# Sample rows in the first prompt pass, weights in 1 MB blocks of 512 columns, and one K projection per head pair

## The chip, the cores and the metric

The kernel runs on the 8 cores of one Trainium2 chip. The batch is divided over them: each core has one prompt of 2048 rows and 16 sample sequences of 4 rows, and all weights. The cores don't talk to each other. The metric is the device time of the slowest core in microseconds (us), as the median of the runs shown.

## The reference

A two-layer decoder step with model width D = 2048 and MLP width 8192, run for a prompt group and for a sample group with the same weights.

```python
# layer 0, recurrent
gate, xr = split(rmsnorm(h) @ w_in, 2)              # w_in (2048, 4096)
xr = causal_conv(xr, conv_state, conv_w, conv_b)    # 4 taps
r, i = sigmoid(block_diag(xr, wa) + ba), sigmoid(block_diag(xr, wx) + bx)   # 16 blocks of 128x128
a = exp(-8 * r * softplus(-lam)); u = sqrt(1 - a * a) * (i * xr)
h_t = a_t * h_(t-1) + u_t                           # scan over time
h = h + (gelu(gate) * hs) @ w_out
h = h + square(relu(rmsnorm(h) @ w_up0)) @ w_dn0    # (2048, 8192), (8192, 2048)
k, v = split(rmsnorm(h) @ w_kv, 2)                  # 4 heads of 64 each; w_kv (2048, 512)
# layer 1, attention over the last 128 positions, with a sink logit per head; 32 query heads of 64
q = rmsnorm(h) @ w_q
p = exp(q k^T / 8 - m) / (sum + exp(sink - m))      # 8 query heads share one k, v head
h = h + (p @ v) @ w_o
h = h + square(relu(rmsnorm(h) @ w_up1)) @ w_dn1
y = rmsnorm(h)
```

The prompt begins with zero states. The sample rows take a convolution state, a recurrent state and a K/V cache of 128 rows for each of the sequences. Outputs are y for both groups, the new states, and the new K and V rows.

## The kernel before

Activations are kept transposed in SBUF: features on the 128 partitions in 16 chunks, rows on the free axis. A pass carries T rows through both layers. `run_pass` (line 492) is called five times: passes 0 to 3 take 512 prompt rows each, pass 4 the core's 64 sample rows (`is_s`, T = 64). The residual stream is `hres` in float32, the bf16 input of the matmuls `xn`; everything else of a pass is laid out by hand in one big tile `U` (class `UV`, line 224).

Matmuls have a 128 x 128 block of weights as the stationary operand and T columns of activations as the moving one. `mm_group` (358) issues a whole accumulation: 16 matmuls for an inner dimension of 2048, 64 for the down-projection. A pass has 5376 such matmuls: 512 of w_in, 256 each of w_out, w_q and w_o, and 1024 each of two up- and two down-projections. `gemm_to_h` (432) does w_out and w_o and adds them to `hres`; `mlp` (445) does up and down: after an up matmul VectorE does relu and the norm's factor (455), ScalarE the square (458). `post_chunk` (416) follows each new chunk of `hres` with its square on ScalarE (376) and, two chunks later, a matmul with ones that sums the squares (380).

The weights come in 85 blocks per pass of 2 MB in bf16 (list `blocks`, 290 to 312; a w_dn block is 8192 rows by 128 columns, the others 2048 by 512, w_in as two parts of 256). There are three slots, `wslot`. `w_acquire` (344) is called before a block is used, and issues loads up to two blocks ahead on the Pool queue; a load waits until the matmuls that read its slot are done. The weights in HBM are float32 and the load casts them. A block with number bi divisible by 3 is read so in pass 0 only, the others in passes 0 and 1; on the last such time SP also stores the bf16 block to the scratch tensor `wscr` (354), from which later passes load it without a cast (333). Of the 425 block loads 141 cast and 284 come from `wscr`; 85 blocks are stored.

The recurrent stage (732 to 743) is a software pipeline over 16 chunks: matmuls of chunk i, then on VectorE the scan of chunk i-3 (708) and the convolution of chunk i-1 (666), its gate matmuls (686) and activations (694). The K projection (785 to 800) computes each of 4 heads twice, once for either half of the partitions, with 64-column weight blocks: 128 matmuls. V (801 to 809) has rows as the stationary operand and streams all 512 columns of w_kv, of which the K half is used only for the last block of the prompt. Attention (`attn_unit`, 856) goes over 32 units of two chunks (four heads) and 128 queries: scores for one or two key blocks (872), exp on ScalarE (878), values and sums of the exponentials (900), and on VectorE sum plus sink (912), reciprocal (916) and two multiplies (918). Each unit is finished before the next is issued. The sample pass has its own attention (937 to 1032), one unit for each of 16 sequences.

Each engine executes its instructions in the order of the program. Dependences are tracked by names of tiles in `Prog`, and become semaphore waits.

The softmax here doesn't subtract the row's maximum and nothing guards it: scores larger than these inputs give would overflow.

## Time and profile before

| what | us |
|---|---|
| median of 3 runs | 7713.69 |
| fastest, slowest of them | 7228.85, 7719.43 |
| profiled execution: span of the slowest core (2) | 7383.0 |
| profiled execution: span of the fastest core (5) | 7094.3 |
| TensorE matmul busy, core 2 | 6128.0 |
| VectorE, ScalarE, GpSimd busy, core 2 | 1823.3, 1561.3, 514.3 |

The profile is of one execution, for which no time other than the spans of its cores is shown. A span goes from the first to the last instruction of a core; a time also has what lies around it. Matmuls overlap, so the mean duration of one (some 400 ns) is not its cost in a stream. "Granted clock" is the share of TensorE's full clock that the chip let through.

### The profile page before, as it was taken

What the parts mean: (1) busy time and instruction counts of PE and PEld (TensorE: products, weight loads), DVE (VectorE), ACT (ScalarE), POOL (GpSimd) and SP (SyncE); (2) the same over time, 40 slices, a digit from 0 to 9 for tenths busy, and PEclk for the clock granted to TensorE, in tenths of its full rate; (3) what the DMA queues carried; (4) which work ended last, traced back from release to release, by engine and by line L of the source; (5) the groups of instructions that cost most, each with busy time, mean ns of one, the idle gap of its engine ahead of it and who ended that gap; (6) DMA issues with size and microseconds to landing.
All of it is one profiled execution on the core that took longest, in us unless ns stands there. A gap on an engine that the chain in (4) does not pass through costs nothing.

```text
span 7383.0 us, 82123 instructions; the slowest of 8 cores (7094.3 to 7383.0 us)
## 1 busy us (share of the span) xinstructions
PE 6128.0 (83%) x32728; PEld 2982.2 (40%) x33176; DVE 1823.3 (25%) x3379; ACT 1561.3 (21%) x2520; POOL 514.3 (7%) x608
## 2 busy tenths in 40 slices
PE   6778788786887888897899989979999899973665
PEld 3333343333333344333344444443444444433545
DVE  6210052102611043103620151035110331023121
ACT  6310012101711012101711031026110121015121
POOL 1002100021001100010000000000000000000000
PEclk8887899898999999888999999977888888875666
DMA  9999959999899957996334313333333123335849
GB/s 157 141 144 139 154 93 130 139 158 178 174 196 200 202 151 143 204 190 176 119 150 151 122 69 149 148 114 113 115 126 125 70 80 126 117 139 172 311 140 332
DMA packets 728559, 1118.41 MB, mean 151 GB/s; under 512 B 467188, under 2 KB 676596, under 8 KB 676596
## 3 DMA queue, kind: packets, MB, share of 16 engines
q0 software_dynamic: 691056, 892.38, 58.7%
q1 hardware_dynamic: 37128, 220.76, 9.0%
q8 instruction: 269, 4.41, 0.2%
q14 instruction: 106, 0.87, 0.0%
HBM read 1213.33 MB, written 196.51 MB: 191 GB/s over the span
## 4 chain that ended last, share of the span: by engine, by line
PE 58%; DMA 21%; issue 7%; DVE 7%; ACT 5%; POOL 1%; another core or an unknown queue 0%; DVEq 0%; ACTq 0%; POOLq 0%; SPq 0%
PE psum L364 53%; DMA sb_wslot<-w_up 9%; DMA sb_wslot<-w_dn 6%; DMA sb_wslot<-wscr 4%; DVE sb_U L916 2%; PE psum L793 1%; POOL sb_wslot L111 1%; DMA sb_wslot<-w_in 1%; PE psum L900 1%; DVE sb_xn L547 1%; ACT sb_U L878 1%; DMA wscr<-sb_wslot 1%; ACT L701 1%; PE psum L380 1%; DVE sb_U L402 1%
## 5 line engine op out<-in xcount | busy, mean ns | idle before, releaser
L364 PE MATMUL psum<-sb_xn,sb_wslot 128*128 128x512 bf16 (+1 forms) x13859 | 2793.4, 368 | 395.3 <-DMA sb_wslot<-w_up 205.1
L364 PE MATMUL psum<-sb_U,sb_wslot 128*128 128x512 bf16 (+1 forms) x12589 | 2575.9, 369 | 336.7 <-DMA sb_wslot<-w_dn 158.2
L364 PEld LDWEIGHTS psum<-sb_xn,sb_wslot 128*128 128x128 bf16 x14080 | 1290.2, 107 | 1883.7 <-issue 978.7
L364 PEld LDWEIGHTS psum<-sb_U,sb_wslot 128*128 128x128 bf16 x12800 | 1167.9, 106 | 1716.1 <-issue 967.9
L455 DVE SCALAR_TENSOR_TENSOR sb_relu_t<-psum,sb_rstd 128x512 f32<-128x512 f32 (+1 forms) x640 | 382.7, 598 | 1919.3 <-PE psum L364 1904.0
L458 ACT ACTIVATE sb_U<-sb_relu_t 128x512 bf16<-128x512 f32 (+1 forms) x640 | 355.2, 556 | 1976.9 <-DVE sb_relu_t L455 1966.8
L376 ACT ACTIVATE sb_sqst<-sb_hres 128x512 bf16<-128x512 f32 (+1 forms) x320 | 177.8, 556 | 2621.8 <-DVE sb_hres L465 2199.3
L465 DVE TENSOR_TENSOR sb_hres<-sb_hres,psum 128x512 f32<-128x512 f32 (+1 forms) x160 | 95.2, 595 | 2233.0 <-PE psum L364 2062.3
L101 POOL DMA_DIRECT2D sb_wslot<-wscr x284 | 151.7, 534 | 4209.1 <-PE psum L364 2439.9
L111 POOL DMA_DIRECT2D sb_wslot<-w_dn x212 | 242.7, 1155 | 917.0 <-issue 489.4
L916 DVE RECIPROCAL sb_U<-sb_U 128x256 f32<-128x256 f32 x128 | 224.4, 1753 | 13.5 <-DVE sb_U L912 0.5
L440 DVE TENSOR_TENSOR sb_hres<-sb_hres,psum 128x512 f32<-128x512 f32 (+1 forms) x160 | 95.2, 595 | 454.7 <-PE psum L364 411.7
L408 ACT ACTIVATE sb_xn<-sb_hres,sb_vecs 128x512 bf16<-128x512 f32 (+1 forms) x280 | 173.7, 632 | 127.8 <-PE psum L364 127.8
L878 ACT ACTIVATE sb_U<-psum 128x512 bf16<-128x512 f32 x248 | 136.4, 595 | 227.1 <-PE psum L872 227.0
L900 PE MATMUL psum<-sb_U,sb_Vpad 128*128 128x128 bf16 x992 | 80.1, 226 | 117.4 <-ACT sb_U L878 117.4
L364 PE MATMUL psum<-sb_U,sb_wgate 128*128 128x512 bf16 (+1 forms) x156 | 45.6, 366 | 150.6 <-DVE sb_U L655 88.8
L678 DVE SCALAR_TENSOR_TENSOR sb_U<-sb_U,sb_vecs 128x512 f32<-128x512 f32 (+1 forms) x240 | 157.9, 658 | 26.1 <-DVE sb_U L678 0.9
L380 PE MATMUL psum<-sb_sqst,sb_onesb 128*128 128x512 bf16 (+1 forms) x316 | 110.4, 359 | 23.6 <-ACT sb_sqst L376 23.3
L364 PE MATMUL psum<-sb_wslot,sb_xn 128*4 128x512 bf16 (+1 forms) x504 | 125.1, 415 | 0.9 <-issue 0.7
L111 POOL DMA_DIRECT2D sb_wslot<-w_up x53 | 60.7, 1145 | 891.7 <-PE psum L364 572.0
L900 PEld LDWEIGHTS psum<-sb_U,sb_Vpad 128*128 128x128 bf16 x992 | 60.3, 100 | 137.3 <-issue 137.3
L649 ACT ACT_TABLE_LOAD x75 | 96.2, 1283 | 74.2 <-PE psum L364 72.7
(136 smaller groups left out, 2733.7 us busy)
## 6 DMA issues: line engine op xcount, KB each, us to landing
sb_wslot<-wscr POOLq DMA_DIRECT2D x284, 2048.0 KB, 9.4
wscr<-sb_wslot SPq DMA_DIRECT2D x85, 2048.0 KB, 14.0
sb_wslot<-w_up POOLq DMA_DIRECT2D x53, 2048.0 KB, 36.1
sb_wslot<-w_dn POOLq DMA_DIRECT2D x212, 512.0 KB, 20.8
sb_wslot<-w_in POOLq DMA_DIRECT2D x26, 1024.0 KB, 31.0
sb_U<-xp SPq DMA_DIRECT2D x16, 1024.0 KB, 9.4
yp<-sb_U SPq DMA_DIRECT2D x16, 1024.0 KB, 4.1
sb_wslot<-w_out POOLq DMA_DIRECT2D x7, 2048.0 KB, 24.1
```

What stands on the lines that cost most here:

```text
L101: self.q[eng].append((waits, lambda e: e.dma_start(out=out, in_=in_), sem, 16))
L111: self.q[eng].append((waits if i == 0 else [], (lambda e, out=out, in_=in_: e.dma_start(out=out, in_=in_)), sem, 16))
L364: ins = e.matmul(out_ap, lhsT=l, rhs=r, start=(i == 0), stop=(i == n - 1))
L376: P.op("act", lambda e: e.activation(out=sq_ap, in_=hres[:, c, 0:T], func=AF.Square), reads=[("h", c)], writes=sq_keys)
L380: P.op("pe", lambda e: e.matmul(psum[:, bank, 0:T], lhsT=onesb[:], rhs=sq_ap, start=(c == 0), stop=(c == NCH - 1)), reads=["onesb"] + sq_k ...
L408: P.op("act", lambda e: e.activation(out=xn[:, c, 0:T], in_=hres[:, c, 0:T], func=AF.Copy, scale=vcol(gv, c)), reads=[("h", c)] + CONST_R, ...
L455: P.op("dve", lambda e, r=r, bank=bank: e.scalar_tensor_tensor(out=relu_t[:, r, 0:T], in0=psum[:, bank, 0:T], scalar=0.0, in1=rstd[:, 0:T] ...
L458: P.op("act", lambda e, r=r, m=m: e.activation(out=hid[m].ap, in_=relu_t[:, r, 0:T], func=AF.Square), reads=[("relu", r)], writes=hid[m].keys)
L678: P.op("dve", lambda e, j=j: e.scalar_tensor_tensor(out=tv(xc.ap), in0=sh_(j), scalar=vcol(V_CW0 + j, c), in1=tv(xc.ap), op0=ALU.mult, op1 ...
L878: P.op("act", lambda e, bank=bank, nk=nk, pt=pt: e.activation(out=pt.ap[0:nk, 0:ncol], in_=psum[0:nk, bank, 0:ncol], func=AF.Exp, scale=0. ...
L900: ins = e.matmul(psum[:, bank, off + ci * nq:off + (ci + 1) * nq], lhsT=lhsT, rhs=Pt[s][kb].ap[0:nk, j * nq:(j + 1) * nq], start=first, st ...
L916: P.op("dve", lambda e: e.reciprocal(out=dn.ap[:, 0:wo], in_=dn.ap[:, 0:wo]), reads=dn.keys, writes=dn.keys)
```

## The change

- The fifth pass is gone. Pass 0 carries the 64 sample rows beside its 512 prompt rows (`S = (pi == 0)`), in tiles of their own (`hres_s`, `xn_s`, `Us`). In `mm16`, which replaces `mm_group`, each stationary block is used twice: for 64 sample columns, into a bank that four chunks share, and then for the 512 prompt columns.
- A weight block is 1024 rows by 512 columns, 1 MB in bf16, for w_dn also; 170 blocks a pass. There are four slots of half the size (4 x 8 KB a partition instead of 3 x 16 KB). `w_pair` acquires two blocks and issues the loads of the next two. The down-projection accumulates four output chunks in four banks over four pairs. The rule for the scratch copy (number divisible by 3) is kept.
- K is projected once per pair of heads, with 128-column weight blocks: 32 matmuls instead of 128; VectorE writes each head to both halves. V streams 256 columns, except for the last block of the prompt.
- Attention is split in `attn_scores` and `attn_pv`, and the scores of the next unit are issued before the values of this one. In pass 0 a sample sequence is worked on between units (`smp_a`, `smp_b`, `smp_c`), every second unit one. The new V rows of the samples go through a scratch tensor `vscr`.
- `rec_sample` does the recurrence of the sample rows four chunks at a time, inside the pipeline of pass 0, in memory of `K2T` and `Us`. The start of pass 0 also loads and transposes the sample inputs and states (`load_T`), and the new states are transposed out after w_out.

```diff
-NSLOT = 3
+NSLOT = 4
+NS = 64
...
-        for pi in passes:
-            for cp in range(8):
-                add_block([(w_in[:, cp * 256:(cp + 1) * 256], 0, 256), (w_in[:, D + cp * 256:D + (cp + 1) * 256], 256, 256)], 16, 512)
...
-            for b in range(16):
-                add_block([(w_dn[0][:, b * 128:(b + 1) * 128], 0, 128)], 64, 128)
...
+    def add_k2048(w, col_parts):
+        for kh in range(2):
+            blocks.append([(w[kh * 1024:(kh + 1) * 1024, c0:c0 + n], off, n) for (c0, off, n) in col_parts])
...
+            for b in range(4):
+                for kb in range(8):
+                    blocks.append([(w_dn[layer][kb * 1024:(kb + 1) * 1024, b * 512:(b + 1) * 512], 0, 512)])
...
+        def w_pair():
+            i = wstate["next"]
+            wstate["next"] += 2
+            while wstate["issued"] < min(len(blocks), i + NSLOT):
+                w_issue(wstate["issued"])
+                wstate["issued"] += 1
...
+        def mm16(wv, wk, c0, rhs, rkeys, out_ap, bank, rhs_s=None, out_s=None, bank_s=None, rkeys_s=(), start=True, stop=True,
+                 start_s=True):
+            for kh in range(2):
+                def fn(e, kh=kh):
+                    ins = None
+                    for k in range(kh * 8, kh * 8 + 8):
+                        l = wv(k, c0, 128)
+                        if rhs_s is not None:
+                            e.matmul(out_s, lhsT=l, rhs=rhs_s(k), start=(start_s and k == 0), stop=(stop and k == 15),
+                                     skip_group_check=True)
+                        ins = e.matmul(out_ap, lhsT=l, rhs=rhs(k), start=(start and k == 0), stop=(stop and k == 15),
+                                       skip_group_check=True)
+                    return ins
...
+            for b in range(4):
+                banks = [next_bank(hold=True) for _ in range(4)]
+                bs_ = next_bank(hold=True) if S else None
+                for q in range(4):
+                    wv, wk = w_pair()
+                    for j in range(4):
+                        mm16(wv, wk, j * 128, lambda k, q=q: hid[q * 16 + k].ap, lambda k, q=q: hid[q * 16 + k].keys,
...
+                if S and i < NCH and i % 4 == 3:
+                    rec_sample(i // 4)
...
+            for gp in range(2):
+                bank = next_bank()
+                bs_ = next_bank() if S else None
+                mm16(wv, wk, gp * 128, XN[0], XN[1], psum[:, bank, :], bank, XNS[0] if S else None,
+                     psum[:, bs_, 0:NS] if S else None, bs_, XNS[1])
...
+            for ui, un in enumerate(units):
+                s = attn_scores(*un)
+                if S:
+                    if ui % 2 == 0:
+                        smp_a(ui // 2)
+                    else:
+                        smp_b(ui // 2)
+                if prev is not None:
+                    attn_pv(*prev)
+                prev = (s,) + un
+                if S and ui % 2 == 0 and ui > 0:
+                    smp_c(ui // 2 - 1)
```

## Rows read from the trace of the kernel before

**Rows 1.** Spans and mean granted clock of the cores.

```profile
core 2: 7383.0 us, clock 0.854
...
core 5: 7094.3 us, clock 0.898
```

**Rows 2.** Core 2 by passes: engines' busy us (instructions), granted clock, DMA share, GB/s.

```profile
0.00:1782.00 1782.00, 1399.00 (x6437) 644.31 (x6550) 416.40 (x677) 334.38 (x488) 225.56 (x205) 0.89 1.06 142
1782.00:3432.00 1650.00, 1381.75 (x6580) 646.03 (x6692) 410.08 (x671) 337.68 (x497) 154.78 (x151) 0.91 0.97 186
3432.00:4891.00 1459.00, 1335.62 (x6581) 637.82 (x6693) 410.14 (x672) 337.97 (x498) 45.18 (x85) 0.95 0.35 129
4891.00:6595.00 1704.00, 1585.56 (x6600) 703.39 (x6711) 414.06 (x674) 341.68 (x501) 45.19 (x85) 0.80 0.29 109
6595.00:7383.00 788.00, 426.02 (x6537) 350.69 (x6535) 172.57 (x688) 209.57 (x538) 43.55 (x82) 0.60 0.66 236
```

**Rows 3.** The same columns for core 0, its passes 0 and 3.

```profile
0.00:1781.00 1781.00, 1605.89 (x6551) 696.54 (x6552) 418.45 (x677) 335.65 (x489) 225.65 (x205) 0.79 1.04 142
...
4917.00:6364.00 1447.00, 1327.26 (x6709) 633.49 (x6708) 410.50 (x674) 339.28 (x500) 45.19 (x85) 0.97 0.35 128
```

**Rows 4.** Weight loads as Pool issues them, in order of time (start us, us).

```profile
267.28 1.14 POOL L111 DMA_DIRECT2D sb_wslot<-w_up  x1 [13.32 <-PE psum L380]
...
558.84 4.58 POOL L111 DMA_DIRECT2D sb_wslot<-w_dn  x4 [21.79 <-PE psum L364]
...
865.00 1.15 POOL L111 DMA_DIRECT2D sb_wslot<-w_kv  x1
...
977.45 1.14 POOL L111 DMA_DIRECT2D sb_wslot<-w_q  x1 [18.96 <-PE psum L364]
991.25 1.14 POOL L111 DMA_DIRECT2D sb_wslot<-w_o  x1 [12.66 <-PE psum L364]
...
3661.44 0.53 POOL L101 DMA_DIRECT2D sb_wslot<-wscr  x1 [14.15 <-PE psum L380]
...
3886.77 0.53 POOL L101 DMA_DIRECT2D sb_wslot<-wscr  x1 [13.28 <-PE psum L364]
```

**Rows 5.** DMA issues: count, KB each, median us from issue to landing.

```profile
sb_wslot<-wscr POOLq DMA_DIRECT2D x284, 2048.0 KB, 9.4
...
sb_wslot<-w_up POOLq DMA_DIRECT2D x53, 2048.0 KB, 36.1
...
sb_wslot<-w_q POOLq DMA_DIRECT2D x6, 2048.0 KB, 19.7
```

**Rows 6.** TensorE in order of time in pass 4 (start us, us, count).

```profile
7173.13 0.67 PE L364 MATMUL psum<-sb_U,sb_wslot 128*128 128x64 bf16 x16
...
7173.67 0.69 PE L364 MATMUL psum<-sb_U,sb_wslot 128*128 128x64 bf16 x16
...
7188.26 3.57 PE L364 MATMUL psum<-sb_xn,sb_wslot 128*128 128x64 bf16 x64 [3.30 <-DMA sb_wslot<-wscr]
```

**Rows 7.** Attention of pass 2, 4247 to 4344: groups by line, busy us, mean ns.

```profile
L916 DVE RECIPROCAL sb_U<-sb_U 128x256 f32<-128x256 f32 x32 | 56.1, 1753 | 3.3
...
L900 PE MATMUL psum<-sb_U,sb_Vpad 128*128 128x128 bf16 x256 | 19.8, 221 | 29.8 <-ACT sb_U L878 29.8
...
L918 DVE TENSOR_TENSOR sb_U<-psum,sb_U 128x128 bf16<-128x128 f32 x63 | 15.5, 287 | 3.3
...
L912 DVE TENSOR_TENSOR sb_U<-psum,sb_dvec 128x256 f32<-128x256 f32 x32 | 13.6, 425 | 5.8 <-PE psum L900 5.8
```

**Rows 8.** Sample attention on VectorE, groups of the whole span.

```profile
L1025 DVE RECIPROCAL sb_U<-sb_U 128x64 f32<-128x64 f32 x16 | 8.8, 553 | 1.8 <-DVE sb_U L1021 0.2
...
L1028 DVE TENSOR_TENSOR sb_U<-psum,sb_U 64x64 bf16<-64x64 f32 x32 | 7.1, 222 | 2.2
...
L972 DVE CAST sb_U<-sb_U 128x512 bf16<-128x512 f32 x16 | 6.8, 423 | 0.5
```

**Rows 9.** Recurrent stage of pass 0, columns as in rows 2.

```profile
62.00:242.00 180.00, 131.84 (x552) 56.65 (x563) 117.19 (x209) 123.98 (x143) 14.85 (x13) 0.86 1.03 148
```

More of the change, by code:

```diff
@@ L349, in w_acquire @@
                 wstate["issued"] += 1
-            parts, kc, nct = blocks[i]
-            s = i % NSLOT
-            pord, bi = divmod(i, NBLK)
-            if pord == conv_pass(bi) and pord < len(passes) - 1:
-                P.dma("sp", wscr[bi], wslot[s][:, :], s_ws[s], reads=[("ws", s, j) for j in range(4)], writes=[("wscr", bi)])
-            view = wslot[s][:, 0:kc * nct].rearrange("p (k n) -> p k n", k=kc)
-            return view, [("ws", s, j) for j in range(4)]
-        def mm_group(out_ap, bank, pairs, reads):
-            n = len(pairs)
+            views = []
@@ new lines, in w_pair @@
+            keys = []
+            for ii in (i, i + 1):
+                s = ii % NSLOT
+                pord, bi = divmod(ii, NBLK)
+                if pord == conv_pass(bi) and pord < len(passes) - 1:
+                    P.dma("sp", wscr[bi], wslot[s][:, :], s_ws[s], reads=[("ws", s)], writes=[("wscr", bi)])
+                views.append(wslot[s][:, :].rearrange("p (k n) -> p k n", k=8))
+                keys.append(("ws", s))
+            return (lambda k, c0, n: views[k // 8][:, k % 8, c0:c0 + n]), keys
@@ new lines, in mm16 @@
+        def mm16(wv, wk, c0, rhs, rkeys, out_ap, bank, rhs_s=None, out_s=None, bank_s=None, rkeys_s=(), start=True, stop=True,
[11 more added lines that the diff above has]
+                    return ins
+                rd = [wk[kh]] + [kk for k in range(kh * 8, kh * 8 + 8) for kk in rkeys(k)]
+                wr = [("ps", bank)]
+                if rhs_s is not None:
+                    rd += list(rkeys_s)
+                    wr.append(("ps", bank_s))
+                P.op("pe", fn, reads=rd, writes=wr)
@@ L361, in fn, with post_s @@
+        def post_s(b, xg):
+            P.op("act", lambda e: e.activation(out=sqst_s[:], in_=hres_s[:, 4 * b:4 * b + 4, :].rearrange("p c t -> p (c t)"),
+                                               func=AF.Square), reads=["h_s"], writes=["sqst_s"])
+            if xg is not None:
+                scale_gs(xg, 4 * b, 4)
+            bank = stats["bank_s"]
             def fn(e):
                 ins = None
-                for i, (l, r) in enumerate(pairs):
-                    ins = e.matmul(out_ap, lhsT=l, rhs=r, start=(i == 0), stop=(i == n - 1))
@@ L432, in gemm_to_h, with h_add @@
-        def gemm_to_h(T, rhs_chunk, rhs_keys, post=None):
+                for j in range(4):
+                    ins = e.matmul(psum[:, bank, 0:NS], lhsT=onesb[:], rhs=sqst_s[:, j * NS:(j + 1) * NS],
+                                   start=(b == 0 and j == 0), stop=(b == 3 and j == 3))
+                return ins
+            P.op("pe", fn, reads=["onesb", "sqst_s"], writes=[("ps", bank)])
+        def h_add(m, bank):
+            P.op("dve", lambda e: e.tensor_tensor(out=hres[:, m, :], in0=hres[:, m, :], in1=psum[:, bank, :], op=ALU.add),
+                 reads=[("h", m)], writes=[("ps", bank), ("h", m)])
@@ new lines, in h_add_s, with post_tail @@
+        def h_add_s(b, bank):
+            P.op("dve", lambda e: e.tensor_tensor(out=hres_s[:, 4 * b:4 * b + 4, :].rearrange("p c t -> p (c t)"),
+                                                  in0=hres_s[:, 4 * b:4 * b + 4, :].rearrange("p c t -> p (c t)"),
+                                                  in1=psum[:, bank, 0:256], op=ALU.add),
+                 reads=["h_s"], writes=[("ps", bank), "h_s"])
+        def post_tail(S):
+            for m in range(NCH - DEFER, NCH):
+                stats_mm(m)
+            stats_finish(S)
```

1087 lines of the change are left out of this document (577 added, 510 removed).

## Prediction

> **What bounds the kernel now.** I read the cores first: core 2 spans 7383.0 us at a mean granted clock of 0.854, core 5 only 7094.3 at 0.898 [rows 1]. Then I cut core 2 at the first output issue of each pass, which gives five stretches [rows 2]: 1782, 1650, 1459, 1704 and 788 us. The reader should see two kinds of pass. Passes 2 and 3 are bound by TensorE: in pass 2 it is busy 1336 of 1459 us while the DMA engines are used at 0.35. Passes 0 and 1 do the same matmuls with DMA share 1.06 and 0.97 and take 323 and 191 us longer: there the float32 weights are read and cast. Pass 4 has one eighth of the rows, yet moves all weights again at 236 GB/s and takes 788 us, at a granted clock of 0.60. Pass 3 is longer than pass 2 by its clock alone: 0.80 against 0.97 for core 0 in its pass 3, which took 1447 us [rows 3].
>
> The weight queue shows the same by blocks [rows 4]. In pass 0 the first up-projection issues 16 blocks in 291.6 us (267.28 to 558.84), 18.2 each, and the down-projection 16 in 306.2, 19.1 each. In pass 2 it is 16 in 225.3, or 14.1, which is TensorE's pace (64 matmuls). In pass 0 the query and output projections too go at TensorE's pace, 13.8 us (977.45 to 991.25), since three slots let them run ahead. A block of w_up lands 36.1 us after its issue, with two or three in flight; one of w_q, nearly alone, after 19.7; one from the bf16 copy after 9.4 [rows 5].
>
> **The change, part by part,** against core 2's span of 7383.
>
> Fifth pass. From 6595 only the output of pass 3 remains; 18 us for it is an estimate (four issues and one landing). Removed: 788 - 18 = 770.
>
> Sample columns in pass 0. Each of 5376 large matmuls gets a 64-column one ahead of it with its own weight load. In pass 4 such pairs of load and matmul run from 7173.13 to 7173.67, sixteen of a group and one for the statistics, which is 32 to 33 ns each; after a DMA wait, at the lower clock, 64 take 3.57 us or 55 ns [rows 6]. I take 33 ns, since here a 512-column matmul stands between them. A block costs 14.1 + 64 x 0.033 = 16.2 us. The bounds are nothing (load and matmul in the shadow of the DMA wait) and 5376 x 55 ns = 296 us, if all is exposed.
>
> Slots and blocks. Two pairs replace three blocks, so the load of pair n+1 starts when pair n-1 has been used, and has one pair's matmuls to hide behind. When a load takes longer than that, two loads overlap in flight, and the queue has nothing for the time from a free slot to the first data. Call that 3 us, an estimate from two issues of 1.14 us [rows 4] and their signals. With P the matmuls of a pair and C the transfer (18.2, the pace of w_up), a pair takes (P + 3 + C) / 2 = (16.2 + 3 + 18.2) / 2 = 18.7 us in pass 0. That is +0.5 for each of 32 up blocks, -0.4 for each of 32 down blocks (19.1 before; their rows of 512 bytes become 2 KB, as w_up has), and +4.6 for each of the 13 of w_out, w_kv, w_q and w_o. Sum 16 - 13 + 60 = +63. Pass 1 has 191 / 85 = 2.2 us a block over pass 2, so C about 16.6; (14.1 + 3 + 16.6) / 2 = 16.9, +0.3 for 64 blocks and +2.8 for 13: about +55, of which I take 48, as some of those blocks hide behind attention. In passes 2 and 3 a pair lands in 9.4 us and has 14.1: nothing, and once that cover is gone (a landing above 14) half the excess per pair. The bounds of this step are 0, where 18.2 was only the old queue's pace, and the price in the second rival.
>
> The 512-byte rows of w_dn cost 5% against w_up's (19.1 to 18.2). The Trainium skill ("DMA: Bandwidth & Descriptors", Specifications) asks for at least 512 bytes per transfer for line rate, since below it the engine reads, modifies and writes; the cast rows of w_dn land as 256 bytes. By that rule alone the down stage would gain far more than the 13 us above. The trace agrees in sign only.
>
> K and V. K takes 32 instead of 128 matmuls a pass, at 0.216 us by the pace of the projections (13.8 / 64): 96 x 0.216 = -21. V streams 256 instead of 512 columns: 64 x 0.108 = -7. At clock 0.80 this is -35 in pass 3. The eight VectorE multiplies for K stay and hide behind V's matmuls.
>
> Attention. Scores of the next unit now go ahead of this unit's values, which looks like 29.8 us saved per pass, TensorE's wait for the exponential. But the unit is bound by VectorE: over 32 units its three groups are busy 13.6 + 56.1 + 15.5 = 85.2 us of some 92 [rows 7], and one unit needs 0.42 + 1.75 + 2 x 0.29 = 2.75 us. I take -3 a pass; bounds 0 and 92 - 85 = 7. In pass 0 a sample rides on every second unit and adds VectorE 0.42 + 0.55 + 4 x 0.22 = 1.85 us [rows 8], times 16 samples: +30.
>
> Recurrence of pass 0: between 62 and 242 VectorE is busy 117.19 of 180 us [rows 9]. Four sample groups add some 42 small operations each at 0.2 to 0.3 us (the L1028 kind), 42 us in all. VectorE runs in order, and the prompt chunk queued behind a group waits, with its gate matmuls behind it. Half is hidden by the wait for w_in: +20, bounds 0 and 42.
>
> Start and end of pass 0: twelve groups of transposes with copies and one normalization before the first matmul, +12; new transposes out, +17; both estimates from copies of 0.2 to 0.4 us, bounds 0 and 60. Reads of vscr wait for its write, many units ahead: nothing.
>
> Sums: pass 0 1782 + 63 + 12 + 20 + 30 - 3 - 28 + 17 = 1893; pass 1 1650 + 48 - 31 = 1667; pass 2 1459 - 31 = 1428; pass 3 1704 - 38 = 1666; end 18. Span 6672, 711 less than 7383. The median of the runs shown, 7713.69, stands 331 above that span, which is more than lies around a program (the fastest run, 7228.85, is 134 above core 5's span). So it holds executions at lower clocks than the profiled one. Carrying the 331 over gives 7003.
>
> **The rivals.**
>
> 1. Lower clock in all passes. Core 0 had 0.79 in pass 0 and 0.97 in pass 3; core 2 the reverse [rows 2, 3]. Fewer waits make the load denser. At 0.80 pass 2 costs 245 more (1704 - 1459). A pair in pass 0 has P = 19.8 and takes 20.5 us, x 85 gives +153; pass 1 in the same way +136. 6672 + 534 = 7206. The old kernel in that case, 1781 + 1650 + 1704 + 1704 + 788 = 7627, comes 87 short of its median; with these, 7293. The old passes 0 and 1 hid this behind DMA (core 0's pass 0 took 1781 at 0.79, core 2's 1782 at 0.89); the new ones have less to hide it. 
>
> 2. Slower: the shallower prefetch is exposed in full. If a pair still needs 36.1 us to land with one pair of cover, a pair takes (36.1 + 1 + 16.2) / 2 = 26.7 us, 8 over the forecast; 85 of them in pass 0 are +680, and in pass 1 (25.6 against 16.9) +740. 8092, or 8423 with the 331. It turns the change slower from 711 / 170 = 4.2 us a pair, a landing of about 30 us. For it speaks that this is the median of w_up; against it that the 36.1 is queueing: w_q, nearly alone, needed 19.7.
>
> 3. High clock throughout, as cores 0 and 5 had in pass 3: pass 3 is 1416, the span 6422, and 6556 with core 5's 134.
>
> 4. Prefetch and sample columns cost nothing, as DMA hides them: 6672 - 111 = 6561, or 6892.
>
> **How the numbers follow.** Forecast 0.40, lower clock 0.20, slower 0.03, high clock 0.25, hidden 0.12. All but the second are faster by more than 2% (about what a measurement of this kernel can tell from no change). Giving 0.02 to mixed cases within 2%, I have faster 0.95, same 0.02, slower 0.03. The range is 6430 to 7300: it takes in both clock cases and a free prefetch, and leaves out the exposed one.
>
> **What would show it.** Four stretches instead of five. Passes 2 and 3 should lose about 31 us each at equal clock, with L793's groups gone; if they lose less, small loads are late. In pass 0 the weight queue should issue a pair every 18 to 19 us in all GEMM stages, query and output too; 16 or less proves the prefetch free, 25 the second rival. VectorE should be nearly full in attention of pass 0 (some 120 us). Landing of 1 MB halves should be well under 30 us. The forecast is wrong if pass 0 grows by over 200 us or shrinks, or if pass 2 does not get shorter.

## Result and profile after

The change took the median from 7700.33 us (five runs, 7228.85 to 7719.43) to 6751.02 (five runs, 6406.34 to 7113.71). The ratio of the executions that can be compared is 0.893, 95% interval 0.869 to 0.917, so the kernel is faster by 8 to 13%. The forecast was 7003, faster, with a range of 6430 to 7300: the direction came true and the median lies inside the range. The times of either kernel spread with the granted clock, so the steps below are held against spans and stretches at like clock.

The profiled execution took 6422.24 us. Its cores, span and mean granted clock:

```profile
core 3: 6419.9 us, clock 0.937
...
core 7: 6363.3 us, clock 0.942
```

Before, core 2 had 7383.0 at 0.854 and core 5 7094.3 at 0.898 [rows 1]. All eight cores now sit at 0.94: this is the clock of the third rival, which gave a span of 6422 us.

Core 3 cut at the first output issue of each pass (us, then busy us of TensorE, its weight loads, VectorE, ScalarE and Pool with instructions, granted clock, DMA share, GB/s), as in [rows 2]:

```profile
0.00:1926.00 1926.00, 1579.40 (x12581) 839.57 (x12582) 522.72 (x1045) 403.56 (x644) 171.25 (x203) 0.91 0.81 135
1926.00:3592.00 1666.00, 1371.80 (x6615) 638.04 (x6614) 413.62 (x676) 342.19 (x500) 137.63 (x178) 0.92 0.86 184
3592.00:4997.00 1405.00, 1302.36 (x6598) 623.43 (x6597) 408.87 (x672) 340.29 (x497) 90.16 (x170) 0.97 0.37 134
4997.00:6405.00 1408.00, 1305.49 (x6615) 625.50 (x6614) 410.06 (x674) 342.02 (x500) 88.05 (x166) 0.97 0.36 129
```

Four stretches are left of five. TensorE's instructions in pass 0 have doubled (12581), and the pass's DMA share has fallen from 1.06 to 0.81. The means over the eight cores are 1925, 1639, 1405 and 1409 us; core 3 is the slowest in pass 1. The right thing to hold them against is a core of before that had the high clock. Core 5 has 1763, 1659, 1442, 1447 and 783 us by the same cut; the four cores 4 to 7, all at high clock, have 1758, 1681, 1442, 1448 and 796 on average. So pass 0 grew by 162 (against the four, 166), pass 1 shrank by 20 (42), passes 2 and 3 by 37 and 38, and 783 became 15. For pass 1 the choice of core matters: core 5 was the fastest of the four.

Pass 0 of core 3 by stages, the same columns: recurrence, w_out, first up and down, K, V and query, attention, w_o, second up and down.

```profile
80.00:345.00 265.00, 154.45 (x1104) 75.76 (x1102) 160.66 (x379) 148.38 (x175) 24.49 (x28) 0.78 0.57 84
345.00:421.00 76.00, 67.87 (x507) 33.67 (x508) 13.30 (x23) 19.54 (x33) 5.24 (x6) 0.92 0.70 97
421.00:1004.00 583.00, 525.32 (x4113) 267.03 (x4111) 70.50 (x110) 66.77 (x119) 55.96 (x64) 0.95 0.93 154
1004.00:1114.00 110.00, 96.67 (x734) 51.03 (x733) 30.90 (x56) 10.74 (x19) 9.62 (x11) 0.92 0.90 146
1114.00:1245.00 131.00, 102.26 (x1243) 81.19 (x1241) 113.69 (x228) 57.78 (x121) 0.87 (x1) 0.89 0.32 68
1245.00:1321.00 76.00, 68.35 (x489) 33.36 (x490) 12.70 (x23) 18.15 (x31) 5.25 (x6) 0.89 0.61 111
1321.00:1906.00 585.00, 532.99 (x4179) 269.25 (x4177) 67.09 (x105) 60.53 (x107) 58.23 (x67) 0.95 0.92 153
```

Core 5 of before, cut in the same way, had 178, 55, 604, 113, 93, 56 and 582 us. These cuts are rough where one stage runs into the next: w_out begins at 336.9, not at 345. The table cuts at TensorE's own matmuls: the first one of w_in, of w_out, of w_o and of each up-projection, and the last one of each down-projection and of the query. It has means in us, with the changes taken before rounding. The forecast is the prediction's, put to the stages (4.6 for each pair of w_out, w_kv, w_q and w_o, and 17 for the new states in w_out):

| stage of pass 0 | before, cores 4 to 7 | after, all cores | change | forecast |
|---|---|---|---|---|
| start, to the first w_in matmul | 62 | 83 | +21 | +12 |
| recurrence (w_in, gates, scan) | 172 | 256 | +84 | +20 |
| w_out, and the new states out | 63 | 95 | +33 | +35 |
| first up and down | 601 | 577 | -24 | +2 |
| K, V and query | 109 | 101 | -8 | -5 |
| attention | 93 | 131 | +38 | +27 |
| w_o | 63 | 87 | +24 | +18 |
| second up and down | 576 | 574 | -2 | +2 |
| end, to the first output | 20 | 21 | +1 | 0 |
| pass 0 | 1758 | 1925 | +166 | +111 |

So the extra time is not in the MLPs, where the weights flow; it is in the recurrence, in attention and in the output projections. Single cores of before differ by 20 us in the first MLP (588 to 608), so its -24 is read as no loss and not as a gain of that size.

The landings, from the DMA issues of the page (KB each, us to landing), answer [rows 5]:

```profile
sb_wslot<-wscr POOLq DMA_DIRECT2D x397, 1024.0 KB, 6.6
...
sb_wslot<-w_up POOLq DMA_DIRECT2D x107, 1024.0 KB, 18.8
sb_wslot<-w_dn POOLq DMA_DIRECT2D x106, 1024.0 KB, 14.3
```

A cast half block lands in 14 to 19 us, well under the 30 at which the second rival would have turned the change slower.

### The profile page after: what moved, and what is told of

It is laid out like the page before. It is cut to its first block, busy times and chain, and to the rows that moved or that the text cites. A ratio compares the mean times of both kernels' runs of the same rounds, so it can differ in the third digit from the quotient of the medians.

```text
span 6419.9 us, 80199 instructions; the slowest of 8 cores (6363.3 to 6419.9 us)
## 1 busy us (share of the span) xinstructions
PE 5563.5 (87%) x32441; PEld 2730.8 (43%) x32441; DVE 1758.7 (27%) x3069; ACT 1431.6 (22%) x2146; POOL 487.1 (8%) x717
## 2 busy tenths in 40 slices
DMA packets 432979, 940.11 MB, mean 146 GB/s; under 512 B 36644, under 2 KB 355684, under 8 KB 355684
## 4 chain that ended last, share of the span: by engine, by line
PE 66%; DMA 15%; DVE 10%; ACT 5%; issue 3%; DVEq 0%; POOL 0%; SPq 0%; ACTq 0%; POOLq 0%
PE psum L381 61%; DMA sb_wslot<-w_up 9%; DMA sb_wslot<-w_dn 3%; DVE sb_U L1031 3%; PE psum L379 2%; DVE sb_xn L638 1%; DVE sb_U L1033 1%; PE psum L408 1%; DMA sb_wslot<-w_in 1%; DVE sb_U L1027 1%; ACT L713 1%; ACT L749 1%; DVE sb_U L1194 1%; DMA sb_wslot<-w_q 1%; DVE sb_U L727 0%
## 5 line engine op out<-in xcount | busy, mean ns | idle before, releaser
L381 PE MATMUL psum<-sb_xn,sb_wslot 128*128 128x512 bf16 x11392 | 2658.8, 389 | 153.4 <-DMA sb_wslot<-w_up 118.8
L381 PE MATMUL psum<-sb_U,sb_wslot 128*128 128x512 bf16 x10240 | 2387.7, 386 | 92.6 <-DMA sb_wslot<-w_dn 47.9
L508 DVE SCALAR_TENSOR_TENSOR sb_relu_t<-psum,sb_rstd 128x512 f32<-128x512 f32 x512 | 353.8, 691 | 1698.7 <-PE psum L381 1698.0
L465 DVE TENSOR_TENSOR sb_hres<-sb_hres,psum 128x512 f32<-128x512 f32 x256 | 176.0, 687 | 2293.0 <-PE psum L381 2286.5
L511 ACT ACTIVATE sb_U<-sb_relu_t 128x512 bf16<-128x512 f32 x512 | 321.9, 629 | 1759.3 <-DVE sb_relu_t L508 1746.8
L442 ACT ACTIVATE sb_sqst<-sb_hres 128x512 bf16<-128x512 f32 x256 | 161.2, 630 | 2263.9 <-DVE sb_hres L465 2263.9
L379 PE MATMUL psum<-sb_xn_s,sb_wslot 128*128 128x64 bf16 x2848 | 561.2, 197 | 95.5 <-DMA sb_wslot<-w_up 81.4
L379 PE MATMUL psum<-sb_Us,sb_wslot 128*128 128x64 bf16 x2560 | 500.4, 195 | 19.2 <-DVE sb_Us L1141 8.0
L379 PEld LDWEIGHTS psum<-sb_xn_s,sb_wslot 128*128 128x128 bf16 x2848 | 284.6, 100 | 104.8 <-issue 104.1
L379 PEld LDWEIGHTS psum<-sb_Us,sb_wslot 128*128 128x128 bf16 x2560 | 253.9, 99 | 26.1 <-issue 20.8
L392 PE MATMUL psum<-sb_U,sb_wgate 128*128 128x512 bf16 x128 | 40.9, 403 | 85.6 <-DVE sb_U L732 82.0
```

The source lines that it names most:

```text
L379: e.matmul(out_s, lhsT=l, rhs=rhs_s(k), start=(start_s and k == 0), stop=(stop and k == 15), skip_group_check=True)
L381: ins = e.matmul(out_ap, lhsT=l, rhs=rhs(k), start=(start and k == 0), stop=(stop and k == 15), skip_group_check=True)
L442: P.op("act", lambda e: e.activation(out=sqst[:, m % 3, :], in_=hres[:, m, :], func=AF.Square), reads=[("h", m)], writes=[("sqst", m % 3)])
L465: P.op("dve", lambda e: e.tensor_tensor(out=hres[:, m, :], in0=hres[:, m, :], in1=psum[:, bank, :], op=ALU.add), reads=[("h", m)], writes= ...
L508: P.op("dve", lambda e, r=r, bank=bank: e.scalar_tensor_tensor(out=relu_t[:, r, :], in0=psum[:, bank, :], scalar=0.0, in1=rstd[:], op0=ALU ...
L511: P.op("act", lambda e, r=r, m=m: e.activation(out=hid[m].ap, in_=relu_t[:, r, :], func=AF.Square), reads=[("relu", r)], writes=hid[m].keys)
```

## Experiments

Where a number for a pass is given, it is the mean over the cores at the high clock (all eight, unless another count stands there), cut at the first output issue.

**Prefetch depth.** Five slots in place of four (the weight view of the V matmuls is bound when they are issued, which five slots need).

```diff
-NSLOT = 4
+NSLOT = 5
```

> Five slots of 1 MB instead of four; nothing left out. Theory of the late loads: half a pair more in flight, w_up of pass 0 from 19.9 to about 18.5, w_up of pass 1 from 18.5 to about 17.5, span 40-80 us shorter in all. Rival, transfer bound: less than 15 us. Passes 2 and 3 unchanged in both.

Core 3, passes 0 and 1:

```profile
0.00:1905.00 1905.00, 1569.78 (x12581) 837.74 (x12582) 523.04 (x1045) 403.31 (x644) 173.31 (x205) 0.92 0.86 137
1905.00:3470.00 1565.00, 1342.56 (x6616) 631.58 (x6615) 413.66 (x676) 341.94 (x500) 136.47 (x177) 0.93 0.92 196
```

Means 1887 and 1571: 38 us off pass 0 and 68 off pass 1, spans 6254 to 6312. Together that is 106, more than either theory gave. In pass 0 the two MLPs gave 35 of the 38; the stages of w_out and w_o stayed at 95 and 86 us. The half slot more does not make a transfer shorter (a w_up half now lands in 25.5 us, queued), it lets the next start earlier. So two pairs in flight were a real price, and in pass 1 larger than the forecast's 48.

**Order within a block.** The upper half of the rows for all four chunks, then the lower half, so that the second half block may land later.

```diff
-for j in range(4): mm16(..., khs=(0, 1))
+for kh in range(2):
+    for j in range(4): mm16(..., khs=(kh,))
```

> In w_out, up, down, query and output stages all four output chunks first use the upper half block, then the lower one, so that a 1 MB slot comes free half a pair earlier; same matmuls, same memory, nothing left out. Theory: with two pairs of slots the loads of passes 0 and 1 start too late, and that sets the pace of w_up (19.9 and 19.2 us a pair in pass 0, 18.5 in pass 1). Then w_up falls to 17.5-18.5, pass 0 by 30-60 us, pass 1 by 20-50 us, passes 2 and 3 stay at 1405 within 5. Rival: the transfer alone sets w_up's pace (its rows lie 32 KB apart, those of w_dn 8 KB); then w_up stays within 0.5 us of its pace and both passes within 15 us.

The times were 6919.71 and 11651.29 us, and the profile is of the latter: core 5 spans 11649.5 us at a granted clock of 0.46, and its 512-column matmuls take 675 ns on average. In the other execution the four cores with clock 0.92 spanned 6341 to 6406, against 6363 to 6420 for the changed kernel. That is a gain of some 20 us at most, in one execution, and it decides nothing between the two theories.

**Sample columns.** Fifteen of sixteen matmuls of each sample accumulation are left out; the sample rows are then incomplete.

```diff
-    if rhs_s is not None:
+    if rhs_s is not None and k == 0:
```

> Of each sixteen 64-column sample matmuls only the first is left, so the sample outputs lack fifteen sixteenths of every inner product; all else stays. 5070 matmuls of 29 ns (245 less 216) are 147 us. Theory: TensorE is close to the bound in pass 0, so a good part comes back: w_dn of pass 0 from 17.1 to 15.5-16.5 a pair, w_up hardly (bound by loads), pass 0 shorter by 50 to 100 us. Rival, all hidden behind the weight transfer: less than 20 us. Rival, all exposed: 140 us or more.

Pass 0 is 1889, 35 us less: neither the 50 to 100 of the theory nor under 20. With 5070 matmuls fewer, that is 7 ns each. The granted clock of the pass fell from 0.91 to 0.88 with them (core 7), so part of what they cost at a fixed clock is hidden in this number. TensorE's waits in pass 0, core 7 (us in total, times, longest), this kernel:

```profile
PE psum L381 <- DMA sb_wslot<-w_up: 115.0, 19, 13.1
...
PE psum L381 <- DMA sb_wslot<-w_dn: 29.3, 12, 4.9
...
PE psum L379 <- DMA sb_wslot<-w_up: 21.5, 7, 5.6
```

and the changed kernel, same core and pass:

```profile
PE psum L379 <- DMA sb_wslot<-w_up: 74.8, 21, 11.0
PE psum L804 <- DVE sb_Us L797: 64.4, 4, 16.1
PE psum L392 <- DVE sb_U L732: 41.8, 5, 17.4
PE psum L459 <- ACT sb_sqst_s L450: 36.5, 16, 2.5
```

The columns that were taken out came back as longer waits for w_up (75 to 136 us, the first and the third line together) and for w_dn (2 to 29). So in the MLP of pass 0 the transfer sets the pace, and most of the sample matmuls' time lies beside it. The other three waits of the second fence are untouched by the edit, and they are the next question.

**The recurrence.** Here TensorE waits 106 us for VectorE. First only the gates of a sample group were moved behind the next chunk's matmuls:

```diff
+if S and i > 3 and i % 4 == 0:      # after st_A_pe(i)
+    rec_sample(i // 4 - 1, 1)       # gates
...
-    rec_sample(i // 4)
+    rec_sample(i // 4, 0)           # convolution
```

> The sample group's gate matmuls and all that follows them are issued one chunk later, after the next chunk's w_in matmuls; nothing is left out. Theory: in the recurrence of pass 0 TensorE loses its time to waiting in order behind those gate matmuls (4 waits of 16 us), and the weight queue stands still with it. Then the stretch from the first w_in matmul (about 80 us) to the first w_out load's release shortens by 50 to 80 us, pass 0 goes from 1926 to 1850-1875, the undisturbed span from about 6395 to 6320-6345. Rival: VectorE's added work is itself the bound of that stage; then the wait moves to the next gate matmuls and less than 20 us come back.

The times were 6934 to 7010 us; four cores at 0.94 had a pass 0 of 1930, no shorter than 1925. My reading, a matmul that blocks the queue behind it, fell as it stood. The trace shows why. These are TensorE's waits for VectorE, core 4, window 80 to 350:

```profile
PE psum L392 <- DVE sb_U L732: 70.4, 5, 17.6
PE psum L806 <- DVE sb_Us L798: 32.1, 3, 16.4
PE psum L379 <- DVE sb_K2T L788: 13.9, 1, 13.9
```

The wait for the sample gates fell from 64.4 to 32.1 us, the wait L392 <- L732 of the next prompt chunk grew from 41.1 to 70.4, and a third came up: 116 us in all, where the changed kernel has 106. Next the gelu too was issued ahead of the prompt's gate activations:

```diff
+if S and i < NCH and i % 4 == 3:    # before st_B1_act(i - 1)
+    rec_sample(i // 4, -1)          # gelu
```

> The gelu of a sample group (ScalarE, 0.38 us) is issued ahead of the four gate activations of the previous prompt chunk, and the sample gates one chunk later. In the changed kernel VectorE's first sample copy waits 7.5 to 7.8 us for this gelu four times (30.3 us), then does 28 operations in 7.9 us, and TensorE stands still 16 us each time. Moving the gates alone had only moved the stall (TensorE's wait for the next chunk's cast rose from 41.1 to 70.4 us). Theory, a serial chain of in-order queues: the 30.3 us go, TensorE's waits for VectorE in the recurrence (106 us in the window from 80 to 350) fall below 50, the w_in stage of pass 0 falls from 277 to 235-250 us and pass 0 from 1926 to 1885-1900. Rival, VectorE's and ScalarE's sum of work (161 and 148 of 270 us) or the cast loads bound it: the stage stays at 270 or more.

Pass 0 is 1905, 20 less, where 26 to 41 were expected. The w_in stage (first w_in issue to first w_out issue) takes 270 us on average, 262 to 276 by core, against 279 (core 3: 277): shorter, but far from 235 to 250. The next expectation gives 272 to 275 for it, which holds for some of the cores only. TensorE's waits for VectorE in core 3, window 80 to 350, fall from 106 to 81 us, not below 50:

```profile
PE psum L392 <- DVE sb_U L732: 70.1, 5, 17.4
PE psum L808 <- DVE sb_Us L800: 10.6, 2, 9.1
```

So the result lies between the theory and its rival.

Where the stall comes from can be seen in the order of time (start us, us), core 3 of the changed kernel:

```profile
183.59 0.63 ACT L753 ACTIVATE sb_U<-sb_U 128x512 f32<-128x512 f32 x1
...
185.53 0.38 ACT L783 ACTIVATE sb_Us<-psum 128x256 f32<-128x256 f32 x1
186.02 0.23 DVE L786 COPY sb_K2T<-psum 128x64 f32<-128x64 f32 x1 [7.54 <-ACT sb_Us L783]
...
193.87 0.29 DVE L797 CAST sb_Us<-sb_K2T 128x256 bf16<-128x256 f32 x1
...
194.31 0.59 PE L804 MATMUL psum<-sb_Us,sb_wgate 128*128 128x64 bf16 x8 [16.06 <-DVE sb_Us L797]
```

VectorE stands 7.5 us for the gelu, does 28 small operations in 7.9 us, and TensorE waits for both. In the kernel with the gelu first the 14 operations behind the gates run from 191.27 to 201.05, and then one prompt chunk takes VectorE from 200.96 to 208.8, or 7.8 us. TensorE's 32 pairs of matmuls for a chunk take 32 x 0.245 = 7.8 us too (0.245 us is the spacing of the 512-column matmuls in pass 0; in passes 2 and 3 it is 0.216). So what a sample group adds to VectorE, work or waiting, is not made up by the chunks behind it. The third version moves the gates behind the prompt's gate matmuls and merges the convolution of four chunks, with broadcast taps:

```diff
-for c in range(4): ... 7 operations over 64 elements
+tensor_copy(xr4[:, :, :, 3:7], px); ... ; tensor_tensor(v4(xc), xr4[:, :, :, 0:4], wb(V_CW0), mult)
+for j in 1..3: tensor_tensor(tj, xr4[:, :, :, j:j + 4], wb(V_CW0 + j), mult); tensor_tensor(xc, xc, tj, add)
```

> The gelu of a sample group first, its gates behind the gate matmuls of the prompt chunk, and the convolution of its four chunks in 11 VectorE operations over 256 elements (taps as broadcast operands) in place of 28 over 64. Moving gelu and gates alone (e10) left the w_in stage at 272-275 us: there VectorE has 28 operations in 7.9 us and 14 in 9.8 us for each group and then 7.8 us for each prompt chunk, as much as TensorE's 32 pairs of matmuls need, so nothing of a group is ever made up. Theory, VectorE's serial time bounds the stage: 28 x 0.28 = 7.9 us become 11 x 0.42 = 4.6, and the 5 us in which VectorE waits within the gates no longer hold up the next chunk's cast; 4 x (3.3 + 5) = 33 us, the stage falls to 240-245 and pass 0 to 1885-1895. Rival, ScalarE (8.0 us of activations and table loads for a chunk) or the loads bound it: 265 or more.

The same window of core 3 and its wait:

```profile
80.00:350.00 270.00, 196.18 (x1411) 96.27 (x1409) 163.03 (x328) 154.37 (x192) 28.18 (x32) 0.85 0.68 99
```

```profile
PE psum L392 <- DVE sb_U L732: 50.9, 8, 12.4
```

The w_in stage falls to 235-239 us and pass 0 to 1882, 43 less than the changed kernel. In equal time 1411 matmuls stand where 1122 stood. The theory of VectorE's serial time holds in its sum: from the version before to this one the recurrence, from matmul to matmul, falls from 240 to 213 us on the mean of the cores, where 33 less were expected, and VectorE's busy time in it from 157 to 146. The two parts of the edit, gates later and fewer operations, were not run apart. The loads did not hold the stage at 265. The clock of the window rose from 0.78 to 0.85 with it, so part of the 43 is clock that the stalls had cost.

**Row distance.** All w_up blocks but the first of a layer are read from w_dn, rows 8 KB apart instead of 32; the up-projections then use other weights.

```diff
-add_k2048(w_up[layer], [(b * 512, 0, 512)])
+blocks.append([(w_dn[layer][r0:r0 + 1024, c0:c0 + 512], 0, 512)])   # b > 0
```

> All w_up blocks but the first of a layer are read from w_dn instead, 1024 rows by 512 columns with rows 8 KB apart in HBM instead of 32 KB; what the up-projection computes is changed by that, its work is not. Theory, the distance of the rows sets the pace of the cast loads: in pass 0 the up stages fall from 20.1 and 19.1 us a pair to the 17.0-17.4 of w_dn, the landing of a pair from 23-25 to 18 us, and in pass 1 from 18.7 to 16.7; 77 us off pass 0 and 65 off pass 1. Rival, what is computed in the stage sets it (a bank, VectorE's relu, ScalarE's square for each chunk): the paces stay within 0.5 us of 20.1, 19.1 and 18.7.

The Pool queue at the start of the first up stage, of down and of K and V, core 3; this kernel, then the changed one:

```profile
404.77 0.87 POOL L112 DMA_DIRECT2D sb_wslot<-w_up  x1 [17.95 <-PE psum L387]
...
676.47 0.87 POOL L112 DMA_DIRECT2D sb_wslot<-w_dn  x1 [12.47 <-PE psum L387]
...
943.73 0.87 POOL L112 DMA_DIRECT2D sb_wslot<-w_kv  x1 [12.84 <-PE psum L387]
```

```profile
400.80 0.88 POOL L112 DMA_DIRECT2D sb_wslot<-w_up  x1 [18.12 <-PE psum L381]
...
722.62 0.87 POOL L112 DMA_DIRECT2D sb_wslot<-w_dn  x1 [20.41 <-PE psum L381]
...
994.41 0.88 POOL L112 DMA_DIRECT2D sb_wslot<-w_kv  x1 [12.85 <-PE psum L381]
```

Sixteen pairs of w_up take 321.8 us in the changed kernel, or 20.1 each, and 271.7, or 17.0, when they are read from the other tensor with its address pattern; w_dn stays at 16.7 to 17.0. Pass 0 falls to 1829 and pass 1 to 1572, together some 161 us. The rival, VectorE's and ScalarE's work on the up chunks, is ruled out: it is all still there.

The Trainium skill ("DMA: Bandwidth & Descriptors", Latency and other measured facts) reports copies that slow down when the row pitch in HBM is a large power of two, from 207 to 164 GB/s between 512 KiB and 2 MiB. These runs agree in kind at far smaller pitches: 8 to 32 KB cost 18% of a pair's pace. Which property of the pattern does it wasn't separated: both distances are powers of two, and no other was run.

**Row size.** Each w_dn block in four DMAs of 128 columns, as 512-byte rows that land as 256 bytes.

```diff
-blocks.append([(w_dn[...][..., b * 512:(b + 1) * 512], 0, 512)])
+blocks.append([(w_dn[...][..., b * 512 + j * 128:...], j * 128, 128) for j in range(4)])
```

> Each w_dn block is cast in four DMAs of 1024 rows by 128 columns, so its rows are 512 bytes in HBM and 256 bytes as bf16, as the kernel before had them; the data is the same. Theory of the forecast (512-byte rows cost 5%): w_dn goes from 17.0-17.4 to about 18 us a pair in pass 0 and from 16.6 to 17.4 in pass 1, +12 to +16 us a pass. Rival, rows below some size cost far more than bytes: 25 us a pair or more, +120 us or more a pass. Second rival, nothing: within 0.3 us a pair.

```profile
0.00:1985.00 1985.00, 1587.31 (x12580) 841.26 (x12581) 522.97 (x1045) 403.83 (x644) 339.40 (x395) 0.90 0.94 131
```

Passes 0 and 1 take 1980 and 1682, +55 and +43, or 1.5 us for each of 64 pairs. The packets under 512 B rise from 36644 to 475908, and Pool's issue time in pass 0 from 171 to 339 us. So rows of the old size cost about 9% of w_dn's pace, not 5%, more than the theory's 12 to 16 us a pass and far less than the rival's 120. The edit also makes four DMAs of each block, and the two are not told apart here. With the old row size pass 1 takes what it took before the change (1682, and 1681 on cores 4 to 7): the longer rows of w_dn are worth as much as all that pass 1 gained.

The Trainium skill ("DMA: Bandwidth & Descriptors", Specifications) asks for 512 bytes for line rate. The trace bears out a small part of that: 9%, and no doubling.

**All stores in pass 0.**

```diff
-            return 0 if bi % 3 == 0 else 1
+            return 0
```

> All 170 blocks are stored to the scratch tensor in pass 0 (57 before), and pass 1 loads everything from there, as passes 2 and 3 do; no other block is cast twice. Pass 1 falls from 1666 to 1405-1415 in every theory. Theory, pass 0 is bound by what a cast load takes and the DMA engines have room beside it (share 0.81): pass 0 grows from 1926 by 50 to 150 us and the span falls to 6210-6310. Rival, a stored block holds its slot until the store has landed (8.7 us) or the DMA engines become full: pass 0 grows by 260 us or more and the span does not fall below 6400.

```profile
0.00:2155.00 2155.00, 1633.94 (x12579) 854.26 (x12580) 522.72 (x1045) 403.36 (x644) 168.76 (x201) 0.88 0.91 176
2155.00:3567.00 1412.00, 1306.36 (x6620) 626.80 (x6619) 413.56 (x676) 342.45 (x501) 90.14 (x170) 0.97 0.38 133
```

Pass 1 falls to 1410 and pass 0 rises to 2151: -228 and +227. Neither theory gave this tie; the price, 2.0 us for each of 113 blocks stored earlier, lies between them. Against this the split of one third to two thirds neither gains nor loses.

**K and attention, each put back alone.** K once per head and half (128 matmuls with 64 columns of weights), and units one after the other:

```diff
-for gp in range(2): mm16(wv, wk, gp * 128, ...)
+for g in range(4):
+    for half in range(2): 16 matmuls with wv(k, g * 64, 64)
```

> K is projected once per head and partition half again (128 matmuls of 512 columns with 64-column weight blocks, in place of 32 with 128). Forecast: 96 matmuls x 0.216 us = +21 us in each of passes 2 and 3 (1405 to 1426) at the high clock. In pass 0 the 64-column matmuls come with it, +24. Rival, part of it was hidden beside the loads of w_q: +5 or less in passes 2 and 3.

```diff
-                if prev is not None:
-                    attn_pv(*prev)
-                prev = (s,) + un
+                attn_pv(s, *un)
```

> Attention units are issued one after the other again: scores, exponentials and values of a unit, then the next. Theory of the forecast, VectorE bounds the stage (85 of 92 us busy before, 94 us long after): passes 2 and 3 grow by 1 to 3 us, 1405 to 1406-1408. Rival, the new order hid TensorE's wait for the exponential (29.8 us a pass before): passes 2 and 3 grow by 15 to 30 us. In pass 0, where the sample units stand between, up to 15 us in either case.

With K put back, pass 2 is 1419 on all cores and pass 3 1426 on six: +15 and +17, or 0.15 to 0.17 us for each of 96 matmuls. But pass 0 is 1928 on six cores, where +24 was expected, and pass 1 is 1642: +3 each. In pass 0 the stage of K, V and query did grow by 21 us (101 to 122), and the two MLPs together took some 20 us less in that execution. Why they did is open.

With attention serial, passes 2 and 3 are 1407 and 1409: +2 and 0. Pass 0 is 1915, 10 less than with the new order, 3 of them in the attention stage (131 to 128). That is one execution, but it gives no sign of a gain there. The groups of attention in pass 2 (busy us, mean ns, idle us before them and its releaser), serial and then changed:

```profile
L979 PE MATMUL psum<-sb_maskb,sb_identb 128*128 128x512 bf16 x62 | 24.8, 400 | 0.0
L1016 PE MATMUL psum<-sb_U,sb_Vpad 128*128 128x128 bf16 x243 | 19.3, 224 | 29.0 <-ACT sb_U L990 29.0
```

```profile
L979 PE MATMUL psum<-sb_maskb,sb_identb 128*128 128x512 bf16 x63 | 23.8, 378 | 22.5 <-DVE sb_U L1033 22.5
...
L1016 PE MATMUL psum<-sb_U,sb_Vpad 128*128 128x128 bf16 x256 | 19.5, 219 | 1.3 <-ACT sb_U L990 1.3
```

The new order removes TensorE's wait for the exponential (29.0 to 1.3 us), and a wait for VectorE stands in its place (0 to 22.5). A reciprocal takes VectorE 1753 ns in both. (The serial window cuts off two of the 32 units.)

**Both gains together.** Five slots and the merged recurrence.

> Five weight slots and the merged sample recurrence (e12) together. Five slots alone gave passes of 1887, 1571, 1405 and 1410 us (means of eight cores), the merged recurrence alone 1882, 1630, 1403 and 1409, the changed kernel 1925, 1639, 1405 and 1409. If the two add: pass 0 1845, pass 1 1565, span 6215 to 6245 at a granted clock of about 0.945. If the w_in loads bound the recurrence once its vector work is shorter, five slots hide that: still 1845. Rival, the two cover the same wait: pass 0 stays at 1880, span 6260 to 6280.

```profile
core 0: 6250.8 us, clock 0.948
core 1: 6247.2 us, clock 0.947
core 2: 6267.5 us, clock 0.947
core 3: 6263.8 us, clock 0.948
```

Pass 0 is 1852 (six cores), pass 1 1570, passes 2 and 3 1405 and 1409: the two add up, within 8 us. The four spans at high clock, 6247 to 6268, lie a little above the 6215 to 6245 expected. Eight executions had a median of 6819.79, against 7228.62 for twelve of the kernel before; two of the eight took 9757 and 12454 us, of which more below. The two in which all cores had a clock above 0.93 took 6277.37 and 6324.06, and the six of before with clocks of 0.90 throughout 7120 to 7199. By the means of these (6300.7 and 7155.8) the version takes 0.881 of the time before, and 114 us less than the changed kernel's 6422.24 and 6406.34.

## Why the prediction was right, and where not

**Fifth pass.** 783 us became 15, so 768 went (770 forecast). This is the whole result to first order; the rest is pass 0 against small gains.

**The clock.** The forecast carried the slower core's pass 3 (1704 us at 0.80) over to the new kernel, and 331 us from span to median. The profiled execution ran at 0.94 throughout, and its span of 6419.9 is the third rival's 6422. In other executions the lower clock of the first rival appears. The profile of the K experiment has it on single stretches, core 0 in pass 3 and core 2 in pass 0:

```profile
4979.00:6605.00 1626.00, 1519.77 (x6581) 687.81 (x6692) 408.68 (x671) 341.65 (x499) 88.04 (x166) 0.83 0.31 112
```

```profile
0.00:2053.00 2053.00, 1758.60 (x12776) 907.53 (x12777) 522.66 (x1045) 403.91 (x645) 171.25 (x203) 0.82 0.77 127
```

They cost 199 us over the 1427 and 125 over the 1928 of the cores at high clock. The first rival priced them at 245 and 153 for a clock of 0.80. These stretches have 0.82 and 0.83. At 0.80 the price is right: core 3 of the first recurrence experiment takes 242 us more in pass 3 than the 1409 at high clock,

```profile
5266.00:6917.00 1651.00, 1564.60 (x6614) 691.81 (x6613) 411.23 (x674) 342.96 (x501) 87.78 (x166) 0.80 0.31 110
```

and cores 4 and 5 of the last experiment take 150 and 156 more in pass 0 (2002 and 2008 against 1852). The median between 6406 and 7114 comes from such stretches, so 7003 was 252 too high mostly by the clock: at the high clock the forecast's own terms give 6422, and the eight cores' spans have a mean of 6392. That the median fell inside the range rests on how often the lower clock came, which no row of the forecast could tell.

One number about the time was wrong: "134 around core 5's span". What lies around a span is 1.5 to 2.4 us (6406.34 against 6404.8; 6422.24 against 6419.9); the 134 compared two different executions.

**Sample columns and prefetch, +63 in pass 0.** The pair's pace was forecast at 18.7 for all GEMM stages. It is 20.1 and 19.1 for w_up and 17.0 and 17.4 for w_dn, where the old blocks, as large as a pair, took 18.2 and 19.1. The MLP stages moved by -24 and -2 us against the forecast's +3 for both together (16 - 13), through two errors of opposite sign. The step "their rows of 512 bytes become 2 KB, as w_up has" took w_dn to w_up's transfer time; it went to 17.2, since its rows also lie nearer to each other than those of w_up. And w_up got slower by 1.4 a pair, which the formula had at 0.5. The formula charged half of a sample column's time, 1.05 us a pair or 89 in all; leaving them out gave 35. The depth of two pairs was underpriced in pass 1 (five slots take 68 off).

The 5% that the forecast gave to the 512-byte rows was read from one stage of one core, 18.2 against 19.1. In core 5 the same stages of before have 19.2 for w_up and 18.1 for w_dn, so one stage of one core could not carry it. The two experiments have both effects apart and larger: 18% between the two distances of rows, in favour of w_dn, and 9% for short rows, against it.

The output projections came out near the forecast, but by luck. Their share of the +60 was a price of the queue, and five slots leave both stages as they are. What TensorE waits for there is told below.

**Recurrence, +20: the step that failed.** "42 us in all ... Half is hidden by the wait for w_in: +20, bounds 0 and 42." The 42 and the half were about right. A group has 43 operations, and VectorE's busy time in the stage rose by 39 us (117 to 156). TensorE waited 16 to 27 us for w_in before, in cores 4 to 7, and not at all after. In core 5 it was:

```profile
PE psum L364 <- DMA sb_wslot<-w_in: 27.1, 2, 17.9
```

What the step left out is the time in which VectorE stands still within a group: four waits of 7.5 us for the gelu, and of the 9.8 us of the 14 operations behind the gates some 5 us each time, for ScalarE above all. A group so holds VectorE for 7.5 + 7.9 + 9.8 = 25 us, 101 in all, and the chunk behind it can't make that up. The stage grew by 84 us at a clock that fell from 0.88 to 0.79. The bound of 42 in the forecast was not a bound. The merged version gave 43 back.

**A wait not forecast.** TensorE waits for the square of the sample columns (L459 <- L450) 16 times, 36.5 us in all: 10 us in each of the two output projections and 7 to 10 in each of the two down-projections. For the prompt the same matmul is deferred by two chunks; for the samples it follows at once. With 256 sample matmuls at 29 ns (0.245 less 0.216), or 7 us, this makes up 17 of the +33 and +24 us of the output projections; the rest is not taken apart here. Deferring it wasn't tried.

**Attention.** -3 forecast, -2 and 0 measured by putting the old order back; VectorE's bound was read rightly from [rows 7]. In pass 0 the samples added 38 us to the stage against 30. VectorE's busy time in it rose by just the 30 (84 to 114), so here too the work was right and the waits were missing.

**K and V.** K was -21 in every pass. It is worth 15 and 17 in passes 2 and 3, and 3 in each of passes 0 and 1, where the forecast took it off in full. V alone wasn't tried. Passes 2 and 3 shrank by 37 and 38 against 31; some 20 us of it are neither K nor attention, 7 of them forecast for V, and the rest is open.

**Pass 1.** 1667 forecast, 17 more than before; 1639 measured, 20 to 42 less than before. The price of 48 for the queue stood without the gain from w_dn's rows, which is 43 by the experiment.

In sum, at the high clock the forecast had 1893, 1667, 1428 and 1416 us for the passes, and 1925, 1639, 1405 and 1409 were measured: 32 short, then 28, 23 and 7 long. Of the 23, 17 lie in the start from core 2, whose pass 2 took 1459 at 0.95 against 1442 at 0.97. That the third rival's span came within 3 us of core 3's is partly these errors cancelling.

## What to carry over

When work is folded into an existing pass, ask for each stage which engine has slack there: the same 64 columns cost 7 ns a matmul on average over the pass, and 84 us in the one stage where VectorE was already nearly as busy as TensorE (117 and 126 us of 172). Busy time alone is no bound for what a chain of small operations costs: add the time in which the engine stands between them for another one. Moving one link of such a chain moved the stall (106 to 116 us); moving two, and then shortening it, gave 20 and 43 us. A saving in TensorE's work counts where TensorE sets the pace: the same K matmuls were worth 15 to 17 us there and 3 in the passes with cast loads. Hold a forecast against stretches at like clock, and keep the clock out of the sum of the work.

## What was not expected of the hardware

Four executions of versions of the new kernel took 9757 to 12454 us, among them the profiled one of the half-block order. There core 5 has a granted clock of 0.46, TensorE was busy 97% of the span, and a 512-column matmul took 675 ns against 389. The record of the clock can't be trusted in it: core 4 has 0.97 and took as long (11552.7 us, 665 ns a matmul), and cores 0 and 1 have 0.55 and took 9783 and 9779. So that TensorE was slow is shown, and the granted clock is not shown to be the reason. No execution of the kernel before did so. The changed kernel itself did not either, in five. What brings it on is open.
